# The order of state scans, head values and ScalarE activations in the mLSTM stretch, and early evictions into eight F buffers in all norms

## The chip, the core and the metric

One core of a Trainium2 chip runs the whole program. The metric is the device time in microseconds of one execution. The engines are TensorE (PE: matmul; PEld: its weight loads), VectorE (DVE), ScalarE (ACT), GpSimd (POOL) and SyncE (SP, which here only issues DMAs). Each engine runs its own instruction list in order, and they meet through semaphores. Matmuls write PSUM, of which this kernel uses eight banks of 128 x 512 f32.

## The reference

Two transformer blocks over 512 tokens of width 1024, in float32. The first one (sparse attention, retention, a squared-ReLU feed-forward) is touched by the change only in its two RMS norms. The second one is:

```
h   = standardize(x) * (1 + sc1) + sh1
xm, om, ip, fp, us, ga, gb = split(h @ w_in + b_in)
xc  = silu(causal_conv4(xm));  q, k = xc @ wq, xc @ wk;  v = xm        # 4 heads, 128 / 128 / 256
hm  = standardize(mlstm(q, k, v, ip, fp))                              # per head
y_a = (hm * gain * sigmoid(om)) @ w_down
ys  = gelu(s5_ssm(us));  val, gate = split(ys @ w_glu);  y_b = val * sigmoid(gate)
x   = layer_norm(alpha * x + (1 + g1) * ((sigmoid(ga) * y_a + sigmoid(gb) * y_b) @ w_mix_out))
h   = standardize(x) * (1 + sc2) + sh2
x   = layer_norm(alpha * x + (1 + g2) * conv_glu_ffn(h))
```

In the mLSTM, with m the running maximum of the gates, s = (q k^T) * exp(D - m) over past tokens, the head's value is (s v) / max(|sum of s|, exp(-m)). The S5 part is a linear state recurrence with 64 complex states for each of 32 groups.

## The kernel before, in words

**Weights.** All weight matrices are cut into 113 tiles of 128 x 2048 (1 MB), in the order of `CHUNKS` (L71). SP loads them into two `raw` slots (`tiles`, L2316; a load waits for the split of the tile two before). ACT rounds a tile to `whi` (`hi_upto`, L889: it waits for the load and for the last product of the tile two before; `take`, L901, splits up to one tile ahead of the product it then evicts). POOL subtracts, `wlo = raw - whi`, in four quarters (L1402). A product of 128 x 512 is then three matmuls for each 128 rows, with the activations split in the same way (`Ahi`/`Alo`, `Bhi`/`Blo`): `gemm` (L428) and `token_gemm` (L459).

**PSUM.** Three pools of banks go round: G (2, for `gemm`), T (4) and O (2). TensorE waits in `bank` (L415) until the user before has freed the bank (`taken`), and consumers wait for `full`.

**The norms.** There are four, s = 0 to 3. Per tile i of 128 tokens: statistics on DVE, square root on ACT (`root`, L907), the scale on DVE (`row_scale`, L1435), the scaled row `N` on ACT (`normed_row`, L913). TensorE turns the row into two banks (`normed_tile`, L453). ACT evicts each bank in four pieces with gain and bias into one of two F buffers (`scaled`, L923), and DVE splits the buffer into `Ahi` and `Alo` (`parts`, L1446). With two buffers an eviction waits for the `parts` of two evictions before (L930). In `normed_out` (L941) all four rows come first, then all evictions; norm 3 has its own loop (L1366 to L1375). In norms 1 and 2 (`rows_of`, L1718) and in norm 3 the rows end in the second half of a `token_gemm`, which sends tile 0's turns before its last piece (L510).

**The S5 part.** Projections `us0` to `us3` go through HBM into runs (`UG`); `run_inputs` (L736) feeds the scans on DVE (`run_states`, L2045, two halves); `run_outputs` (L751, two halves) adds 32 products with `TOEG` and 64 with the scanned states `xs`; `runs_out` (L1178) stores them as `y_runs`, `y_back` loads them as `YC`, `gelus` and DVE's `ys_part` make `YShi`/`YSlo`.

**The spilled projections.** 32 projections `xm`, `om`, `ga`, `gb` (k = 0 to 31) are computed, evicted (L1288), and stored to HBM (`spill`). The other work of the stretch hangs on their number k, in one list for TensorE (L831 to L857) and one for ACT (L1282 to L1343). TensorE: k = 2 `run_inputs`, k = 6 the `aec` transposes of the gate rows, k = 8 and 9 `run_outputs`. DVE's list is written out: `gate_rows` 1, 2, 3 (cumulative sums and maxima of the gates, L2015, with activations of ACT at k = 1, 2, 3 between them), then the two scans, then the heads (L2183 to L2203).

**A head** h starts at b = `HEAD_AT[h]`. On TensorE: k = b `mlstm_front` (the product `nb` and the turns of `XM` to `V`), b+1 `mlstm_qk`, b+2 `mlstm_scores`, b+3 `mlstm_values` (ten products of 256 columns into two O banks, and ten of one column, the denominator, into a T bank), b+5 `mlstm_back` (turns of `H`). On ACT: b+1 `head_in`, `head_qk`, `head_decay`; b+2 `load_so`; b+4 the `silus` of the next head's conv and then `head_rows` (the root and four scaled rows `H`); b+6 `head_high` (`Bhi`). On DVE: `weighted`, `head_low` of the head before, `conv` of the next, `values_out` (statistics and denominators), `conv_out` (`XCh`/`XCl`), `diagonal`, `head_out`.

**After them** come eight steps of `gv`, `gg`, `md` products; the first `md` waits for all of `Bhi`/`Blo`. ACT takes `gv` after DVE's `g8_free`. SP waits for all spills and `heads_done`, loads the gains of the norm, and then for each step two 256 KB gate tiles and one weight tile (L2398 to L2411).

Of the kernel before, what the change touches and what calls it, by code (L numbers as in the profile page):

```python
# [55 lines left out]
HEAD_AT = [13, 17, 22, 26]  # L56
# [105 lines left out]
def build(nc, d, out):  # L162
    ctx = ExitStack()
    with ctx:
# [184 lines left out]
        G2b = at("G2b", [P, D], offY)  # L349

# [61 lines left out]
        def _(pe):  # L412
# [46 lines left out]
            def token_gemm(name, hi, lo, kn, ready, turns=False, s=None):  # L459
# [323 lines left out]
            def mlstm_values(h):  # L783
# [3 lines left out]
                for p in range(2):  # L787
                    ps, where = bank("O")
                    for i in range(2 * p, 2 * p + 2):
                        for j in range(i + 1):  # L790
                            at_ = [0, 512, 896, 1152][j] + (i - j) * P
                            ins = pe.matmul(ps[:, i % 2 * ML_DV:(i % 2 + 1) * ML_DV], W[:, at_:at_ + P],  # L792
                                            V[:, j, 0:ML_DV], start=(j == 0), stop=(j == i))
                    done(ins, f"mn{h}.{p}", where)
                ps, where = bank("T")
                for i in range(NT):
                    for j in range(i + 1):
                        at_ = [0, 512, 896, 1152][j] + (i - j) * P
                        ins = pe.matmul(ps[:, i:i + 1], W[:, at_:at_ + P], V[:, j, ML_DV:ML_DV + 1],
                                        start=(j == 0), stop=(j == i))  # L800
                done(ins, f"den{h}", where)

            def mlstm_back(h):
                for p in range(2):
                    pe.wait_ge(*taken(f"mn{h}.{p}"))
# [25 lines left out]
            for k, name in enumerate(SPILLED):  # L831
# [5 lines left out]
                if k == 6:  # L837

                    pe.wait_ge(sem("ifr_ready"), T.due("ifr_ready"))
                    ps, where = bank("T")  # L840
# [44 lines left out]
        def _(act):  # L885
# [37 lines left out]
            def scaled(i, s):  # L923

                for x in range(2):
# [15 lines left out]
            def normed_out(s, more=None):  # L941

                for i in range(NT):
                    root(i, s)
                    normed_row(i, s)
                    if i == 1 and s:
                        hi_upto(more)
                if s == 0:
                    hi_upto(more)
                    act.wait_ge(sem("par_in"), A.due("par_in", 16))  # L950
                elif s == 2:
                    act.wait_ge(sem("mod_ready"), A.due("mod_ready"))
                for i in range(NT):
                    scaled(i, s)
# [257 lines left out]
            def head_in(h):  # L1212

                for c in range(2):
                    act.wait_ge(*full(f"v{h}.{c}"))
                    ps = bank_of(f"v{h}.{c}")
                    if h and c == 0:
                        act.wait_ge(*full(f"den{h - 1}"))
# [22 lines left out]
            def head_rows(h):  # L1241
# [7 lines left out]
                for i in range(NT):  # L1249
                    ps = bank_of(f"mn{h}.{i // 2}")  # L1250
                    ins = act.activation(H[:, i, :], ps[:, i % 2 * ML_DV:(i % 2 + 1) * ML_DV], ACT.Identity,
                                         scale=sd[:, i:i + 1], bias=nmr[:, i:i + 1])
                    if i % 2:
                        ins.then_inc(taken(f"mn{h}.{i // 2}")[0], 1)
# [27 lines left out]
            for k, name in enumerate(SPILLED + [""]):  # L1282
# [20 lines left out]
                if k == 2:  # L1303
# [3 lines left out]
                if k == 3:  # L1307
# [5 lines left out]
                if k == 8:  # L1313
# [11 lines left out]
                if k in (16, 18):  # L1325
                    gelus(k - 16)
                    gelus(k - 15)
# [1236 lines left out]
```

## Time and profile before

| | |
|---|---|
| median of 3 runs | 1675.78 us (1673.12 to 1678.27) |
| the profiled execution | 1674.36 us, its span 1672.4 us |
| mean granted TensorE clock | 0.945 |
| busy: PE, DVE, POOL, ACT | 91%, 53%, 38%, 35% |
| from 820 to 1140 us (S5 and mLSTM) | PE 289.6 of 320 us, clock 0.91 |

### The profile page before, as it was taken

The page shows a single profiled execution, that of the slowest core. Times are in us where ns is not written, and L with a number is a line of the kernel's source. Part 1 is how long each engine was busy: PE and PEld are TensorE (multiplying, and loading weights), DVE is VectorE, ACT ScalarE, POOL GpSimd, SP SyncE. Part 2 cuts the span into 40 slices and gives each one's busy share as a digit, 9 for nine tenths or more (in the row PEclk, how much of TensorE's full clock was granted, in tenths as well). Part 3 has the DMA queues.
Part 4 walks back from the last instruction along what each step waited for, and adds up shares of the span by engine and source line. Part 5 has one row for each costly group of instructions (what it writes and reads, how often), then busy time and mean ns, then how long its engine had stood idle before and what let it go on. Part 6 is the DMA issues. An engine that isn't in the chain of part 4 may idle for free. (4 is left out here: it accounts for less than half of the span.)

```text
span 1672.4 us, 19643 instructions
## 1 busy us (share of the span) xinstructions
PE 1525.9 (91%) x7216; PEld 1226.2 (73%) x7216; DVE 879.7 (53%) x1484; ACT 582.6 (35%) x856; POOL 643.0 (38%) x456
## 2 busy tenths in 40 slices
PE   4999989787999999997998999988994999999996
PEld 3776855676888788875877777777883888888885
DVE  4672378625858777397462255424548332333337
ACT  4332377115222121215341463444426332232231
POOL 2432200032655545562542224224551434544442
PEclk9999989898999999997997998998996999999998
DMA  7222000042655545222452633224421222223221
GB/s 273 88 92 78 26 26 2 1 164 97 212 189 198 205 151 189 101 76 82 113 149 78 173 103 131 89 87 171 138 76 76 76 101 101 84 93 105 97 101 51
DMA packets 48182, 185.72 MB, mean 111 GB/s; under 512 B 12960, under 2 KB 14112, under 8 KB 33248
## 3 DMA queue, kind: packets, MB, share of 16 engines
q1 hardware_dynamic: 30240, 165.53, 28.1%
q10 hardware_dynamic: 17856, 19.01, 4.1%
q8 instruction: 58, 0.95, 0.2%
q14 instruction: 28, 0.23, 0.0%
HBM read 169.71 MB, written 12.58 MB: 109 GB/s over the span
## 5 line engine op out<-in xcount | busy, mean ns | idle before, releaser
L1402 POOL TENSOR_TENSOR wlo<-raw,whi 128x512 fp32r<-128x512 f32 x448 | 637.3, 1453 | 997.0 <-ACT whi L898 997.0
L441 PE MATMUL bank<-Ahi,whi 128*128 128x512 f32 x1088 | 440.9, 405 | 22.0 <-issue 8.5
L442 PE MATMUL bank<-Alo,whi 128*128 128x512 f32 x1088 | 431.4, 397 | 0.0
L443 PE MATMUL bank<-Ahi,wlo 128*128 128x512 f32 x1088 | 431.2, 396 | 0.0
L898 ACT ACTIVATE whi<-raw 128x2048 fp32r<-128x2048 f32 x113 | 216.4, 1915 | 279.2 <-PE bank L471 216.9
L441 PEld LDWEIGHTS bank<-Ahi,whi 128*128 128x128 f32 x1088 | 210.1, 193 | 71.6 <-issue 17.4
L442 PEld LDWEIGHTS bank<-Alo,whi 128*128 128x128 f32 x1088 | 210.0, 193 | 45.1 <-issue 2.4
L443 PEld LDWEIGHTS bank<-Ahi,wlo 128*128 128x128 f32 x1088 | 208.9, 192 | 44.9
L469 PE MATMUL bank<-whi,Bhi 128*128 128x512 f32 x496 | 195.3, 394 | 5.6 <-POOL wlo L1402 5.6
L471 PE MATMUL bank<-whi,Blo 128*128 128x512 f32 x496 | 194.3, 392 | 0.0
L470 PE MATMUL bank<-wlo,Bhi 128*128 128x512 f32 x496 | 194.2, 392 | 0.0
L469 PEld LDWEIGHTS bank<-whi,Bhi 128*128 128x128 f32 x496 | 94.1, 190 | 27.0 <-POOL wlo L1402 7.4
L471 PEld LDWEIGHTS bank<-whi,Blo 128*128 128x128 f32 x496 | 93.8, 189 | 19.7
L470 PEld LDWEIGHTS bank<-wlo,Bhi 128*128 128x128 f32 x496 | 94.1, 190 | 19.2
L1742 DVE CUSTOM_DVE_ANT_0 junk<-adaw,cB 128x1024 f32<-128x1024 f32 x48 | 79.2, 1650 | 21.6 <-DMA adaw<-in_ada 16.6
L2283 DVE TENSOR_SCALAR FG<-GP,par 128x512 f32<-128x512 f32 x22 | 12.0, 546 | 147.8 <-ACT GP L1383 147.8
L450 PE MATMUL bank<-con,N 128*128 128x128 f32 x128 | 28.4, 381 | 49.9 <-ACT F L938 19.3
L1951 DVE TENSOR_TENSOR G<-G 128x512 f32<-128x512 f32 x32 | 33.4, 1044 | 62.3 <-ACT G L1114 62.3
L1288 ACT ACTIVATE stage<-bank,par 128x512 f32<-128x512 f32 x32 | 21.9, 684 | 125.7 <-PE bank L443 99.2
L1114 ACT ACTIVATE G<-bank 128x512 f32<-128x512 f32 x32 | 19.1, 598 | 130.4 <-PE bank L443 130.4
L450 PEld LDWEIGHTS bank<-con,N 128*128 128x128 f32 x128 | 20.7, 194 | 56.9 <-issue 43.9
L1466 DVE TENSOR_TENSOR X<-X,bank 128x512 f32<-128x512 f32 x40 | 27.5, 688 | 45.0 <-PE bank L471 43.9
(379 smaller groups left out, 1928.3 us busy)
## 6 DMA issues: line engine op xcount, KB each, us to landing
raw<-in_ws SPq DMA_DIRECT2D x113, 1024.0 KB, 5.0
adaw<-in_ada SPq DMA_DIRECT2D x48, 512.0 KB, 4.8
spill<-stage ACTq DMA_DIRECT2D x32, 256.0 KB, 2.0
X<-in_x SPq DMA_DIRECT2D x8, 512.0 KB, 6.2
gates<-spill SPq DMA_DIRECT2D x16, 256.0 KB, 2.9
w1k<-in_w1k SPq DMA_DIRECT2D x1, 2048.0 KB, 16.0
w1v<-in_w1v SPq DMA_DIRECT2D x1, 2048.0 KB, 20.2
XM<-spill ACTq DMA_DIRECT2D x8, 256.0 KB, 4.5
```

The source lines that it names most:

```text
L441: pe.matmul(ps[:], wh, hi[:, k], start=(k == 0), stop=False)
L442: pe.matmul(ps[:], wh, lo[:, k], start=False, stop=False)
L443: ins = pe.matmul(ps[:], wl, hi[:, k], start=False, stop=(k == kn - 1))
L450: ins = pe.transpose(ps[0:cols, i * width:i * width + rows], s, ident[0:rows, 0:rows])
L469: pe.matmul(ps[:], h, wh, start=(k == 0), stop=False)
L470: pe.matmul(ps[:], h, wl, start=False, stop=False)
L471: return pe.matmul(ps[:], l, wh, start=False, stop=stop)
L898: act.activation(whi[n % 2][:], raw[n % RAW][:], ACT.Copy).then_inc(sem("hi_split"), 1)
L1402: pool.tensor_tensor(wlo[slot][:, part], raw[slot][:, part], rd(whi[slot][:, part]), ALU.subtract).then_inc(sem("lo_split"), 1)
L1466: tt(x, x, ps[:], ALU.add).then_inc(taken(n)[0], 1)
L1742: dve.tensor_tensor_reduce(junk[:], adaw[t % 3][:], cB[:], 1.0, 0.0, ALU.mult, ALU.add, mod[:, t:t + 1]).then_inc(sem("ada_used"), 1)
L1951: tt(r[:], r[:], r[:], ALU.mult).then_inc(sem("dve_step"), 1)
```

## The change

Norms: eight buffers `FN` instead of two, at addresses free at that time. `scaled(i - 1)` follows `normed_row(i)` on ACT, the weight split comes after row 0 (norms 1, 2) or row 3 (norm 0), tile 0's turns are issued one piece earlier, DVE's `row_scale` of norm 0 follows the next tile's statistics, and norm 3 evicts three banks and splits tile 0 before its last row. mLSTM stretch: heads at 12, 17, 22, 27; scans before `gate_rows` 2 and 3, with ACT's part of them at k = 4 and 8 and `aec` at k = 9 (a bank of O) and 10; the wait for `xs_ready` behind the `TOEG` products; values and denominator in one product of 257 columns into a bank for each tile; `gelus` at 15 and 20, `head_rows` before `silus`, `ys_part` 2 and 3 after head 1's values; head 3's turn behind `gg0`, and one more weight tile loaded ahead of the spill wait.

```diff
-HEAD_AT = [13, 17, 22, 26]
+HEAD_AT = [12, 17, 22, 27]
...
+        firsts = {0: [offU + 2048 * q for q in range(8)], 1: [offX8 + 4096 + 2048 * q for q in range(8)]}
+        firsts[2] = firsts[1]
+        firsts[3] = [offU, offU + 2048] + [offU + 6144 + 2048 * q for q in range(6)]
+        FN = [[at(f"FN{n}_{q}", [P, S], firsts[n][q]) for q in range(8)] for n in range(4)]
...
             def token_gemm(name, hi, lo, kn, ready, turns=False, s=None):
...
-                    if turns and (q, i) == (1, 2):
+                    if turns and (q, i) == (1, 1):
                         normed_tile(s, 0)
...
             def run_outputs(half):
...
-                    pe.wait_ge(sem("xs_ready"), T.due("xs_ready"))
...
+                if half == 0:
+                    pe.wait_ge(sem("xs_ready"), T.due("xs_ready"))
                 for k in ks:
...
             def mlstm_values(h):
...
-                for p in range(2):
-                    ps, where = bank("O")
...
                 for i in range(NT):
+                    ps, where = bank("O" if i < 2 else "T")
                     for j in range(i + 1):
                         at_ = [0, 512, 896, 1152][j] + (i - j) * P
-                        ins = pe.matmul(ps[:, i:i + 1], W[:, at_:at_ + P], V[:, j, ML_DV:ML_DV + 1],
+                        ins = pe.matmul(ps[:, 0:ML_DV + 1], W[:, at_:at_ + P], V[:, j, :],
                                         start=(j == 0), stop=(j == i))
-                done(ins, f"den{h}", where)
+                    done(ins, f"mn{h}.{i}", where)
...
             for k, name in enumerate(SPILLED):
...
-                if k == 6:
+                if k == 9:
                     pe.wait_ge(sem("ifr_ready"), T.due("ifr_ready"))
-                    ps, where = bank("T")
+                    ps, where = bank("O")
...
                 gemm(f"gg{n}", YShi, YSlo)
                 if n == 0:
+                    mlstm_back(ML_H - 1)
                     pe.wait_ge(sem("B_ready"), T.due("B_ready", 8))
...
-            def scaled(i, s):
+            def scaled(i, s, halves=(0, 1)):
...
-                    if i:
-                        act.wait_ge(sem("A_ready"), 8 * s + 2 * (i - 1) + x + 1)
-                        f, p4 = Fb[x][:, c * P:(c + 1) * P], ps[:, c * P:(c + 1) * P]
+                        f, p4 = FN[s][2 * i + x][:, c * P:(c + 1) * P], ps[:, c * P:(c + 1) * P]
...
             def normed_out(s, more=None):
...
-                    if i == 1 and s:
+                    if i == 0 and s:
                         hi_upto(more)
...
+                    if i == NT - 1 and s == 0:
+                        hi_upto(more)
+                    if i:
+                        scaled(i - 1, s)
+                scaled(NT - 1, s)
...
             for k, name in enumerate(SPILLED + [""]):
...
-                if k == 2:
+                if k == 4:
                     act.wait_ge(sem("if_d"), A.due("if_d"))
                     act.activation(gr[0][0:4], IF[32:36], ACT.Copy).then_inc(sem("if_a"), 1)
-                if k == 3:
+                if k == 8:
                     act.wait_ge(sem("if_d"), A.due("if_d"))
                     act.activation(gr[0][0:4], gr[0][0:4], ACT.Exp).then_inc(sem("ifr_ready"), 1)
-                if k == 8:
+                if k == 10:
                     act.wait_ge(*full("aec"))
...
-                if k in (16, 18):
-                    gelus(k - 16)
-                    gelus(k - 15)
+                if k in (15, 20):
+                    gelus(0 if k == 15 else 2)
+                    gelus(1 if k == 15 else 3)
...
-                    if k == b + 6 or (k == len(SPILLED) and b + 6 >= k):
+                    if k == b + 6:
                         head_high(h)
...
                     if k == b + 4:
+                        head_rows(h)
                         if h < ML_H - 1:
                             silus(h + 1)
-                        head_rows(h)
+            hi_upto(last_tile(INDEX["gv0"]) + 1)
+            head_high(ML_H - 1)
...
                 normed_row(i, 3)
...
-            for i in range(NT):
-                scaled(i, 3)
+                if i == 1:
+                    scaled(0, 3)
+                if i == 2:
+                    scaled(1, 3, (0,))
+            scaled(1, 3, (1,))
+            scaled(2, 3)
+            scaled(3, 3)
...
                 row_stats(i, True)
-                row_scale(i, True)
+                if i:
+                    row_scale(i - 1, True)
+            row_scale(NT - 1, True)
...
-            for part in (1, 2, 3):
-                gate_rows(part)
+            gate_rows(1)
...
             run_states(0)
+            gate_rows(2)
             run_states(1)
             dve.sem_inc(sem("xs_ready"), 1)
+            gate_rows(3)
...
             def values_out(h):
...
+                    dve.wait_ge(*full(f"mn{h}.{i}"))
+                    ps = bank_of(f"mn{h}.{i}")
+                    den_ = ps[:, ML_DV:ML_DV + 1]
+                    ts(dd[:, i:i + 1], den_, -1.0, AEC[:, 1, i, h:h + 1], ALU.mult, ALU.max).then_inc(sem("dve_step"), 1)
+                    dve.bn_stats(st4[:, i, 0, :], ps[:, 0:ML_DV])
+                    dve.wait_ge(sem("dve_step"), v.did("dve_step"))
+                    ins = tt(dd[:, 4 + i:5 + i], dd[:, i:i + 1], den_, ALU.max)
...
                 values_out(h)
-                if h == 0:
-                    ys_part(0)
-                    ys_part(1)
+                if h < 2:
+                    ys_part(2 * h)
+                    ys_part(2 * h + 1)
...
-                if h == 0:
-                    ys_part(2)
-                    ys_part(3)
...
             dve.sem_inc(sem("gb_used"), 1)
+            parts(3, 0)
             again_scale(NT - 1)
-            for i in range(NT):
+            for i in range(1, NT):
                 parts(3, i)
...
-            n_heads = n_s5
+            n_heads = n_s5 + 1
+            tiles(n_s5, n_heads)
             whole_spill()
```

## Rows read from the trace of the kernel before

**Rows 1.** Stretches: length, busy time of PE, PEld, DVE, ACT, POOL, granted clock, DMA
```profile
883.09:888.62 5.53, 0.00 (x0) 0.03 (x1) 5.30 (x5) 0.77 (x2) 3.51 (x3) 0.68 0.29 76
...
888.62:902.64 14.02, 14.02 (x97) 13.78 (x97) 0.00 (x0) 0.00 (x0) 0.00 (x0) 0.50 0.16 65
...
902.64:909.54 6.90, 6.90 (x26) 5.60 (x25) 0.00 (x0) 0.00 (x0) 0.00 (x0) 0.79 0.00 0
...
916.87:933.49 16.62, 16.61 (x74) 13.44 (x72) 0.09 (x3) 2.64 (x5) 0.37 (x1) 1.00 0.61 139
...
909.54:916.87 7.33, 7.33 (x97) 7.19 (x95) 0.00 (x0) 2.48 (x2) 4.57 (x4) 1.00 0.09 36
...
935.72:943.07 7.35, 7.35 (x25) 5.63 (x25) 4.84 (x4) 3.60 (x3) 5.53 (x4) 0.77 0.53 167
...
962.05:1118.11 156.06, 147.52 (x663) 119.01 (x662) 70.96 (x142) 76.69 (x107) 49.51 (x36) 0.93 0.28 95
...
1124.50:1134.55 10.05, 0.00 (x0) 0.03 (x1) 0.00 (x0) 2.47 (x3) 0.50 (x1) 0.64 0.99 373
```

**Rows 2.** Timeline of DVE: start, length, the first instruction of the scans
```profile
857.85 0.69 DVE L2053 TENSOR_TENSOR zz<-bank,ctab 128x512 f32<-128x512 f32 x1
```

**Rows 3.** Who TensorE waited for, 820 to 1140 us
```profile
PE bank L450 <- ACT H L1251: 6.2, 3, 2.2
...
PE bank L441 <- DVE XCl L2107: 1.6, 1, 1.6
...
PE bank L441 <- ACT QK L1239: 0.8, 1, 0.8
```

**Rows 4.** Timeline and one source line: tile 69, and the `Blo` of the heads
```profile
1120.59 1.42 DVE L2180 TENSOR_TENSOR Blo<-F,Bhi 128x512 fp32r<-128x512 f32 x2 [0.24 <-DVE F L2171]
...
L2180 DVE TENSOR_TENSOR Blo<-F,Bhi x8: 693/1476/1666, 1006.8 to 1121.3; 128x512 fp32r<-128x512 f32 x8
...
1132.06 1.91 ACT L898 ACTIVATE whi<-raw 128x2048 fp32r<-128x2048 f32 x1 [10.92 <-DMA raw<-in_ws]
```

**Rows 5.** Timeline: projection 10's eviction, the first conv, head 0's last `XCl`
```profile
922.64 0.69 ACT L1288 ACTIVATE stage<-bank,par 128x512 f32<-128x512 f32 x1 [10.41 <-PE bank L443]
...
938.16 0.94 DVE L2003 TENSOR_SCALAR CA<-XM,par 128x512 f32<-128x512 f32 x1 [21.02 <-DMA XM<-spill]
...
949.05 0.69 DVE L2107 TENSOR_TENSOR XCl<-CA,XCh 128x512 fp32r<-128x512 f32 x1
```

**Rows 6.** Source line L1207, the `silus`: duration min/median/max in ns
```profile
L1207 ACT ACTIVATE CA<-CA x8: 632/633/635, 946.4 to 1077.2; 128x512 f32<-128x512 f32 x8
...
L1207 ACT ACT_TABLE_LOAD  x4: 1283/1283/1283, 938.1 to 1075.3; - x4
```

**Rows 7.** Chain of waits: head 3's value products and one-column products
```profile
1100.65 4.32 PE bank L792 x20
...
1104.97 2.12 PE bank L799 x20
```

**Rows 8.** Norms: `parts` by source line, evictions, each norm's first projection
```profile
L1456 DVE TENSOR_TENSOR Alo<-F,Ahi x32: 692/693/1639, 20.8 to 1294.4; 128x512 fp32r<-128x512 f32 x32
...
16.21 1.15 ACT L917 ACTIVATE N<-X,sd 128x1024 f32<-128x1024 f32 x1 [0.30 <-DVE sd L1438]
...
402.72 0.77 PE L441 MATMUL bank<-Ahi,whi 128*128 128x512 f32 x1 [3.98 <-issue]
...
759.32 1.09 PE L450 MATMUL bank<-con,N 128*128 128x128 f32 x8
...
780.13 0.77 PE L441 MATMUL bank<-Ahi,whi 128*128 128x512 f32 x1 [4.66 <-DVE Alo L1456]
...
1282.43 11.44 ACT L938 ACTIVATE F<-bank,mod 128x128 f32<-128x128 f32 x32
...
1293.83 0.77 PE bank L441
```

**Rows 9.** DMA issues: the gate loads, and their median time to landing
```profile
gates<-spill SPq DMA_DIRECT2D x16, 256.0 KB, 2.9
```

More of the change, by code:

```diff
@@ L786, in mlstm_values @@
                 pe.wait_ge(sem("mw_ready"), T.due("mw_ready", NT))
-                for p in range(2):
-                    ps, where = bank("O")
[L789 to L794, printed above, removed]
-                ps, where = bank("T")
                 for i in range(NT):
+                    ps, where = bank("O" if i < 2 else "T")
                     for j in range(i + 1):
                         at_ = [0, 512, 896, 1152][j] + (i - j) * P
-                        ins = pe.matmul(ps[:, i:i + 1], W[:, at_:at_ + P], V[:, j, ML_DV:ML_DV + 1],
+                        ins = pe.matmul(ps[:, 0:ML_DV + 1], W[:, at_:at_ + P], V[:, j, :],
                                         start=(j == 0), stop=(j == i))
-                done(ins, f"den{h}", where)
+                    done(ins, f"mn{h}.{i}", where)
             def mlstm_back(h):
-                for p in range(2):
-                    pe.wait_ge(*taken(f"mn{h}.{p}"))
+                for i in range(NT):
+                    pe.wait_ge(*taken(f"mn{h}.{i}"))
                 for c in range(2):
@@ L836, in _ @@
                     run_outputs(k - 8)
-                if k == 6:
+                if k == 9:
                     pe.wait_ge(sem("ifr_ready"), T.due("ifr_ready"))
-                    ps, where = bank("T")
+                    ps, where = bank("O")
                     for x in range(2):
@@ L921, in normed_row @@
                 ins.then_inc(sem("norm_rows"), 1)
-            def scaled(i, s):
-                for x in range(2):
+            def scaled(i, s, halves=(0, 1)):
+                for x in halves:
                     n = f"xT{s}.{i}.{x}"
@@ L945, in normed_out @@
                     normed_row(i, s)
-                    if i == 1 and s:
+                    if i == 0 and s:
                         hi_upto(more)
[L948 to L952, printed above, removed]
-                for i in range(NT):
-                    scaled(i, s)
+                    if i == 0 and s == 0:
+                        act.wait_ge(sem("par_in"), A.due("par_in", 16))
+                    if i == 0 and s == 2:
+                        act.wait_ge(sem("mod_ready"), A.due("mod_ready"))
+                    if i == NT - 1 and s == 0:
[3 more added lines that the diff above has]
+                scaled(NT - 1, s)
             def through(name):
@@ L1217, in head_in @@
                     if h and c == 0:
-                        act.wait_ge(*full(f"den{h - 1}"))
+                        act.wait_ge(*full(f"mn{h - 1}.{NT - 1}"))
                     act.activation(V[:, :, c * P:(c + 1) * P], ps[:].rearrange("p (i c) -> p i c", i=NT),
@@ L1249, in head_rows @@
                 for i in range(NT):
[L1250 to L1254, printed above, removed]
+                    n = f"mn{h}.{i}"
+                    act.activation(H[:, i, :], bank_of(n)[:, 0:ML_DV], ACT.Identity, scale=sd[:, i:i + 1],
+                                   bias=nmr[:, i:i + 1]).then_inc(taken(n)[0], 1)
             def head_high(h):
@@ L2132, in values_out @@
                 for i in range(NT):
[L2133 to L2139 removed]
+                    dve.wait_ge(*full(f"mn{h}.{i}"))
[5 more added lines that the diff above has]
+                    ins = tt(dd[:, 4 + i:5 + i], dd[:, i:i + 1], den_, ALU.max)
+                ins.then_inc(sem("dve_step"), 1)
                 dve.wait_ge(sem("dve_step"), v.did("dve_step"))
[L2141 to L2142 removed]
                 dve.reciprocal(dd[:, 4:8], dd[:, 4:8]).then_inc(sem("dve_step"), 1)
@@ L2272, in _ @@
             dve.sem_inc(sem("gb_used"), 1)
+            parts(3, 0)
             again_scale(NT - 1)
-            for i in range(NT):
+            for i in range(1, NT):
                 parts(3, i)
```

11 lines of the change are left out of this document (1 added, 10 removed).

## The prediction

> **What bounds the kernel now.** The page first: TensorE is busy 91% of the span, every other engine at most 53%. So time can only come from three places: where TensorE waits, where it runs at its lower clock, and work of its own that is removed. The table of stretches gives all three for the region the change touches. The chain of waits says who ended each wait, and the timeline says what stood in that engine's queue.
>
> The dearest place is the state scan. After the first `om` projection TensorE waits 5.53 us for `xs_ready`. Then the 96 small products of `run_outputs(0)` take 14.02 us at a granted clock of 0.50, where the same work in `run_outputs(1)` takes 7.33 us at 1.00. The projection after them needs 6.90 us instead of 5.54 (16.62 us for three at full clock) [rows 1]. Behind it: DVE starts the scans at 857.85 though the products that feed the first scan end at about 847, because all three `gate_rows` parts stand in front of them [rows 2].
>
> From head 0's values to the last spilled projection, 156.06 us hold 147.52 us of work [rows 1]: 8.5 us are waits. Most end on `H` (6.2 us, three heads), two short ones on `XCl` and `QK` [rows 3]. After them TensorE repeats instructions at half rate (the clock of the stretch is 0.93). I count about 8.6 us of that: 29 wide matmuls at 0.43 instead of 0.23 us, and some 3 us on turns and products. Before the first `md` product it waits 10.05 us for a G bank [rows 1]: ACT takes `gv0` only after splitting tile 69, whose load SP issues after `heads_done` [rows 4].
>
> **The sum, part by part**, against the profiled execution of 1674.4 us (median of the runs: 1675.8, so 1.4 us above it).
>
> 1. *Scans before gate rows 2 and 3, the skip products ahead of the `xs_ready` wait.* The scan of a half costs at most 17 us (871.8 to 888.5, half of it beside POOL) and gate rows 2 at most 4. From 847 this gives `xs_ready` at 876 to 885. TensorE asks for it at 882.4 + 3.5 = 886 (the end of projection 8 less the 0.66 of the `aec` transposes, which move behind it, and half of `run_outputs`). ACT's new wait at projection 4 for the cumulative sum ends near 864, before projection 5 is complete (865.9). Its wait at projection 8 for gate rows 3 ends by 890, while TensorE is in `run_outputs(0)`; the transposes that need it come at about 903. So the wait goes, and the clock stays up: 5.53 + (14.02 - 7.33) + (6.90 - 5.54) = **-13.6**.
> 2. *Head 0 one projection earlier (13 to 12).* This adds a wait. ACT issues the loads of `XM` behind eight `y_runs` stores; they land 15.5 us after projection 10 ended (922.6 to 938.16) [rows 5], and nothing of this moves. TensorE now wants `XM` 11.9 us after it: two projections of 5.5, one product of 0.9. It waits 3.9 us. Then it has one projection before it needs `XCl`, 27 us after projection 10 (949.7) [rows 5]: 3.2 us more. Each wait is followed by a stretch at the low clock, 1.5 to 1.8 us lost (today, after a wait of 2.23, the projection from 935.72 took 7.35 instead of 5.54 [rows 1]). Lost 10.2, against 4.4 that this stretch loses now: **+5.8**. Ends: 0 and +12 (both waits twice as long).
> 3. *`silus` behind `head_rows`, heads 5 projections apart.* `H` comes 2.6 us earlier (a table load of 1.28 and two activations of 0.63 [rows 6]), and ACT needs 4.9 us from the full projection to `H` (eviction 0.7, table load 1.28, root 0.2, DVE's scale and mean 0.8, four rows 1.9) where TensorE computes 5.5. The scaled `CA` comes later, but `mlstm_qk` is now a projection further off. New: `head_high` stands in front of `V` and `QK` at three hand-overs, some 1.0 us each like today's 0.8 [rows 3]. Head 3's hand-over and head 2's rows have a weight split (1.9) in front too, 1.9 and 1.2. With 1 to 2 us of low clock, 7 of the 17 us stay: **-10**. Ends: 0 and -17.
> 4. *The 257th column in the value products.* The ten one-column products cost 2.12 us a head on the chain, ten of 256 columns 4.32 [rows 7]; one column more is 0.4% of that. 4 x 2.1 = **-8.4**. `values_out` gets about 0.9 us longer on DVE; it has 17 us between the scores and the root and needs 11 to 16 for weights, `head_low` and conv, 4 for itself. It hides, just. No row has 257 columns: if the form needed a second pass, 4 x 4.3 = +17, the other end.
> 5. *Tile 69 before the spill wait, head 3 turned back behind `gg0`.* The load and split are now done early. What is late next is `B_ready`: from the turn of head 3 at 1118.0 it takes 4 us (to 1122.0), up to 5.5 now, because POOL splits tile 69 meanwhile and the two `Blo` subtractions cost 1.6 each instead of 0.7 [rows 4]. Then `g8_free` releases `gv0`. `md0` starts 5.5 + 1.0 (the turn) + 4.5 + 0.7 (`gv0`) = 11.7 us after `gb7` instead of 16.4: **-4.7**. Ends: -1 and -7.
> 6. *The norms.* Eight buffers take away the ping-pong of ACT and DVE over two. In norm 3, 12 of 32 evictions move ahead of the last row; 20 of 0.36 us are left after it, but `parts(3, 0)` pushes that row back 0.8: start 1290.3 instead of 1293.83 [rows 8], **-3.6**. In norm 1 the last row comes at 392.3 and DVE has seven halves of 1.17 us to split: 400.5 instead of 402.72, **-2.2**. In norm 2 ACT serves 32 evictions of 0.36 us in any order, and TensorE reaches the early `normed_tile` before its row exists: it idles from 756.4 to 759.3 and loses clock: 780.5 instead of 780.13 [rows 8], **+0.4**. In norm 0 `row_scale(0)` waits for the second tile's statistics, row 3 comes at 19.6 instead of 16.2, and the splits of tiles 0 and 1 fall into the time of `parts`. Beside a POOL subtraction DVE's 0.69 us takes 1.64 [rows 8], and a cast and subtraction together 3.0 instead of 1.17. I take three halves at 3 us: 34.8 instead of 31.75, **+3**, ends -1.5 and +4. Together **-2.4**.
>
> The row shows that DVE and POOL stretch each other. The Trainium skill (SBUF - State Buffer, Who interferes with whom) says why: a VectorE instruction with two SBUF inputs and a GpSimd one that reads SBUF exclude each other for the whole instruction, first come, first served. By that rule, with the longer POOL instruction first each time, norm 0 would cost the +4 end; with DVE first, little.
>
> Sum: -13.6 + 5.8 - 10 - 8.4 - 4.7 - 2.4 = -33.3, so **1641 us**.
>
> **The rivals.**
> A: *the forecast*, 1641, chance 0.62.
> B: *the head stretch stays chained.* ACT and DVE pass `XM`, `CA`, `V`, `QK`, `H` in an order just as tight as before, and every wait over 2 us costs low clock after it. Steps 2, 3 and 5 then give +12, 0 and -1: -13.6 + 12 + 0 - 8.4 - 1 - 2.4 = -13, 1661; half of that way is 1651. For it: the conv of head 1 took 10 us beside POOL, and DVE has under 1 us to spare there. Against: most waits had `silus` or a load in front of them. Chance 0.16.
> C: *the `XM` wait does not come, and the hand-overs clear.* Step 2 gives 0, step 3 -17: 1628. For it: today's stretch there loses 4.4 us for a similar cause. Against: the loads' place in ACT's queue is not changed. Chance 0.15.
> D: *257 columns double the value products*: 1641 + 17 = 1658. The present products already read `V` with rows of 257 elements at full rate. Chance 0.04.
> E: *slower.* SP's loop now issues `tiles(n_heads + n)` one tile further, so the pair of gate loads for step n + 1 stands behind a wait for the split of tile 68 + n. If that split came after the gates are needed, each of the 8 gated steps would pay a landing of 2.9 us [rows 9], a sigmoid of 1.05 and 1.8 of low clock: 8 x 5.8 = +46, 1687. It decides once the split of tile 68 + n ends later than `g8_free` of the step before. The split is asked for with `gv` of step n - 1, about when `g8_free` of n - 2 comes, and the windows from 1160 to 1240 have TensorE busy throughout. Chance 0.03.
>
> The range is 1628 to 1656: it takes in C and half of B, and leaves out its far end, D and E. A measurement of this kernel can tell about 0.3%, 5 us, from no change. A, C and D are faster by more; of B's 0.16 I give 0.02 to no change and 0.01 to slower, should its waits be worse than drawn. With E: faster 0.94, same 0.02, slower 0.04.
>
> **What would show it.** Step 1: no wait at the skip products and `run_outputs(0)` at clock 1.00 in about 7.4 us. Step 2: a wait of about 4 us ended by the `XM` load, and one of 3 us by `XCl`. Step 3: no wait on `H`, short ones on `QK`. Step 4: 80 product records of 257 columns (0.38 us each), no one-column ones. Step 5: no wait on tile 69, about 5 us before `md0`. Step 6: first projections at about 35 us in norm 0, 2 us earlier after norm 1, 3.6 after norm 3, unchanged after norm 2. The forecast is wrong if TensorE still waits over 2 us at each hand-over, or if the `XM` wait is missing.

## The result, and the profile after

The changed kernel takes 1645.08 us (median of four runs, 1643.17 to 1652.11), the kernel before 1677.03 beside it. The ratio is 0.9819, 95% interval 0.9801 to 0.9838: 30.4 us faster (27.2 to 33.4), where 33.3 was the sum. The profiled execution took 1643.61 us, its span is 1641.7, against 1674.36 and 1672.4.

The stretches of the changed kernel that answer to [rows 1]: length, busy time of PE, PEld, DVE, ACT, POOL, granted clock, DMA.
```profile
886.06:893.46 7.40, 7.40 (x98) 7.26 (x96) 6.64 (x4) 2.60 (x3) 6.54 (x4) 1.00 0.56 177
893.46:898.96 5.50, 5.50 (x24) 4.54 (x25) 0.00 (x0) 0.00 (x0) 0.00 (x0) 1.00 0.57 194
898.96:906.36 7.40, 7.40 (x98) 7.26 (x97) 0.00 (x0) 3.77 (x3) 3.31 (x3) 1.00 0.09 35
...
930.03:936.79 6.76, 6.76 (x24) 5.11 (x23) 6.44 (x7) 0.38 (x1) 3.38 (x3) 0.80 0.31 101
...
951.94:1100.85 148.91, 142.29 (x628) 113.72 (x627) 71.46 (x166) 78.59 (x109) 47.90 (x36) 0.99 0.33 114
1101.88:1106.79 4.91, 0.00 (x1) 0.03 (x1) 4.25 (x5) 2.28 (x5) 4.49 (x3) 1.00 0.00 0
```
The 96 products of `run_outputs(0)` now take 7.40 us at full clock with no wait ahead of them (14.02 at 0.50 before), the projection behind them 5.50 (6.90). The fifth row runs from head 0's scores to head 3's turn, with one projection more than the long row of [rows 1] and the two products of `gv0` and `gg0`: it lies at clock 0.99 instead of 0.93. The last row is the wait before the first `md` product, 4.91 instead of 10.05.

Who TensorE waited for, 820 to 1140 us (us in total, times, longest), against [rows 3]:
```profile
PE bank L445 <- DVE Blo L2185: 4.9, 1, 4.9
PE bank L750 <- DMA UG<-u_runs: 3.9, 1, 3.9
PE bank L454 <- DMA XM<-spill: 3.5, 1, 3.5
PE bank L445 <- DVE XCl L2113: 3.1, 1, 3.1
PE bank L454 <- ACT H L1249: 2.7, 1, 2.7
PE bank L445 <- ACT QK L1237: 2.7, 3, 1.1
PE bank L445 <- ACT stage L1284: 1.2, 1, 1.2
```
The waits on `XM` and `XCl` that step 2 priced are there, and of the three on `H` one is left. The products of one head's values (each product with 257 columns leaves two records, so ten of them are x20), and from the timeline the first projection behind each norm and the one new wait, in norm 2:
```profile
L796 PE MATMUL bank<-V,W x20: 377/380/383, 1085.5 to 1089.6; 128*128 128x257 f32 x20
```
```profile
35.10 0.80 PE L445 MATMUL bank<-Ahi,whi 128*128 128x512 f32 x1 [12.70 <-DVE Alo L1459]
...
407.32 0.76 PE L445 MATMUL bank<-Ahi,whi 128*128 128x512 f32 x1 [5.25 <-issue]
...
761.66 1.66 PE L454 MATMUL bank<-con,N 128*128 128x128 f32 x8 [2.29 <-ACT N L917]
...
782.97 0.76 PE L445 MATMUL bank<-Ahi,whi 128*128 128x512 f32 x1 [5.27 <-DVE Alo L1459]
...
1263.08 0.76 PE L445 MATMUL bank<-Ahi,whi 128*128 128x512 f32 x1 [4.39 <-issue]
```

### The profile page after: what moved, and what is told of

Its sections match the earlier page's. It is cut to its first block and busy times, and to the rows that moved or that the text cites. A ratio compares the mean times of both kernels' runs of the same rounds, so it can differ in the third digit from the quotient of the medians.

```text
span 1641.7 us, 19484 instructions
## 1 busy us (share of the span) xinstructions
PE 1502.7 (92%) x7136; PEld 1208.2 (74%) x7136; DVE 890.2 (54%) x1508; ACT 582.4 (35%) x857; POOL 645.4 (39%) x456
## 5 line engine op out<-in xcount | busy, mean ns | idle before, releaser
L454 PE MATMUL bank<-con,N 128*128 128x128 f32 x128 | 24.8, 356 | 40.2 <-ACT N L917 20.6
L1284 ACT ACTIVATE stage<-bank,par 128x512 f32<-128x512 f32 x32 | 21.9, 684 | 86.8 <-PE bank L447 63.6
```

The source lines that it names most:

```text
L454: ins = pe.transpose(ps[0:cols, i * width:i * width + rows], s, ident[0:rows, 0:rows])
```

## The experiments

Each kernel was timed in five rounds beside the kernel before on the same chip, and chips differ between groups. So ratios are compared, and differences in us are ratios times 1677 us.

**The four parts, each alone on the kernel before.**

`norms_only` is the hunks of the norms. 

> The kernel before with the norms' part of the change alone (FN buffers, evictions behind each row, early turns, late row_scale of norm 0). My sum: -2.4 us against before (norm 0 +3, norm 1 -2.2, norm 2 +0.4, norm 3 -3.6), so 1673 to 1674 us. The two traces so far show something that the sum has no term for: from the first projection (31.75 before, 35.10 after) to wout the changed kernel loses 2.9 us more in code that nothing touches. If that belongs to the late start of norm 0 (the clock falls at other places), it shows here too: the stretch from the first projection to wout takes 309.1 us instead of 306.2, and the whole is +0.5 rather than -2.4. If it comes with the mLSTM part (which is later in time, so it could only be chance), this stretch takes 306.2 as before.

Measured: 0.9979 (0.9964 to 0.9994), -3.5 us. Norm 0 starts the first projection at 35.69 (+3.9), norm 1 gives 1.7, norm 2 costs 0.35, norm 3 gives 3.5 (all from the start of the work that leads to the norm, against the same distance before), together -0.9. From the first projection to `wout` it takes 307.2 us: neither the 309.1 of the one theory nor the 306.2 of the other. What ten profiles say of this stretch stands further down.

`scans_only`:
```diff
-            for part in (1, 2, 3):
-                gate_rows(part)
+            gate_rows(1)
...
             run_states(0)
+            gate_rows(2)
             run_states(1)
             dve.sem_inc(sem("xs_ready"), 1)
+            gate_rows(3)
```
with ACT's steps at k = 4 and 8, `aec` behind projection 9, and the `xs_ready` wait behind the `TOEG` products. 

> The kernel before with the scans ahead of gate rows 2 and 3, ACT's gate steps at k = 4 and 8, aec behind projection 9, and the xs_ready wait behind the TOEG products; nothing else. Parts add up: -13.6 us, 1662 us; no wait before the scanned-state products, run_outputs(0) at clock 1.00. Rival (the time is given back later, since the heads and y_runs then come at the same distance behind DVE's shorter slack): -8 us or less, with longer waits on XM, XCl and H than the kernel before has.

Measured: 0.9916 (0.9899 to 0.9933), -14.1 us; parts add up. `run_outputs(0)` of this kernel and the projection behind it, in the table of stretches:
```profile
887.04:894.44 7.40, 7.40 (x98) 7.26 (x96) 6.65 (x4) 2.60 (x3) 6.55 (x4) 1.00 0.56 178
894.44:899.94 5.50, 5.50 (x25) 4.54 (x25) 0.00 (x0) 0.00 (x0) 0.00 (x0) 1.00 0.56 194
```
The waits at the heads are as before (6.1 us on `H`): nothing is given back.

`values_only`:
```diff
-                            ins = pe.matmul(ps[:, i % 2 * ML_DV:(i % 2 + 1) * ML_DV], W[:, at_:at_ + P],
-                                            V[:, j, 0:ML_DV], start=(j == 0), stop=(j == i))
+                        ins = pe.matmul(ps[:, 0:ML_DV + 1], W[:, at_:at_ + P], V[:, j, :],
+                                        start=(j == 0), stop=(j == i))
```
with a bank for each of the four sums, two of O and two of T. 

> The kernel before with the 257-column value products alone (and what reads them: values_out, head_rows). Parts add up: 4 x 2.1 = -8.4 us, 1667 us. Rival (the hand-overs behind it are bound by DVE and ACT, not by TensorE): the four H waits grow by what TensorE saves, 2 us each, and the whole gains under 2 us.

Measured: 1.0024 (1.0009 to 1.0038), 4.0 us slower (1.5 to 6.4), worse than either theory. The products did become 2.1 us shorter for each head. Who TensorE waited for in this kernel, and from its timeline ACT's rows of head 0 and the turn of head 1's second bank of `V`:
```profile
PE bank L450 <- ACT H L1243: 17.1, 3, 7.4
```
```profile
987.68 1.93 ACT L1243 ACTIVATE H<-bank,nmr,sd 128x256 f32<-128x256 f32 x4 [0.77 <-DVE nmr L2150]
...
989.20 1.11 PE L450 MATMUL bank<-con,XM 128*128 128x128 f32 x4 [7.39 <-ACT H L1243]
```
Look at the tile: it is the turn of `XM` that waits, and what ends the wait is a row of `H` of the head before. Of the four T banks two now hold `mn0.2` and `mn0.3` until these rows are written; `nb1` and `v1.0` take the other two, and `v1.1` has none. It happens where heads are 4 projections apart: at head 1 and at head 3, 7.4 us each. The prediction priced the products and DVE's longer `values_out`, not the banks.

`heads_tail_only` is `HEAD_AT` 12, 17, 22, 27, `head_rows` before `silus`, `gelus`, `ys_part`, head 3's turn and tile 69. 

> The kernel before with HEAD_AT 12, 17, 22, 27, head_rows before silus, gelus at 15 and 20, ys_part 2 and 3 after head 1, head 3's turn behind gg0 and tile 69 ahead of the spill wait. My steps 2, 3 and 5: +5.8 - 10 - 4.7 = -8.9 us, 1667 us. Rival (the steps need the scans' and the values' part to work, because the one-column products and the late y_runs give DVE and ACT time): the sum of the four parts run singly is then less than the -30.7 us of the whole change by over 5 us.

Measured: 0.9991 (0.998 to 1.0002), -1.5 us. Apart from the 5.5 us for `xs_ready`, the waits are nearly those of the changed kernel (2.6 on `H`, 2.4 on `XM`, 4.2 on `XCl`, 4.9 on `Blo`), so steps 2 and 5 are at work, and still almost nothing is won. The four parts singly give -3.5 - 14.1 + 4.0 - 1.5 = -15.1, half of the -30.4 of the whole. So it came as the rival has it.

**Heads, tail and values together.** `heads_values` has the last two, without norms and scans. 

> The kernel before with the heads', the tail's and the values' part, without the scans and the norms. Singly the heads' and tail's part brought -1.5 us and the values' part +4. The trace of the values' part alone shows why it lost: mn2 and mn3 now sit in two of the four T banks until the rows of H are written, and with heads 4 projections apart the second turn of V (head 1 and head 3) waits for such a bank, 7.4 us each. It also shows TensorE at full clock after the products (two projections in 11.28 us instead of 12.77). Theory of the bank: with heads 5 apart both waits go, and each head gives 2.1 + 1.5 us: -1.5 - 4 x 3.6 = -16 us, about 1661 us, no gap at a turn of V. Rival (parts add): +2.5 us, 1679 us.

Measured: 0.9914 (0.9898 to 0.993), -14.4 us, where the two singly sum to +2.5. No turn of `V` waits. Norms, scans and this: -3.5 - 14.1 - 14.4 = -32.0, the whole within its interval. So the missing half lay between these two parts. The stretch from head 0's first scores to the wait before the first `md` product, in the kernel before, `values_only`, `heads_tail_only`, `heads_values` and the changed kernel:
```profile
959.97:1124.49 164.52, 155.98 (x699) 125.32 (x697) 75.45 (x149) 80.43 (x110) 49.51 (x36) 0.94 0.29 100
```
```profile
962.56:1127.90 165.34, 145.15 (x619) 115.25 (x617) 75.79 (x173) 80.54 (x110) 48.52 (x36) 0.93 0.28 98
```
```profile
964.02:1131.26 167.24, 160.77 (x723) 129.65 (x721) 70.02 (x144) 81.44 (x110) 47.76 (x36) 0.95 0.30 106
```
```profile
961.37:1116.41 155.04, 148.39 (x643) 117.71 (x641) 72.74 (x168) 81.54 (x110) 47.84 (x36) 0.97 0.32 114
```
```profile
949.63:1101.88 152.25, 145.63 (x643) 116.03 (x641) 72.75 (x168) 81.56 (x110) 47.90 (x36) 0.99 0.33 116
```
The last three hold one projection (5.5 us) more. Length less PE's busy time gives the waits; the granted clock while PE is busy gives what its lower level costs (1 less the clock, times the time); the products are 8.4 us shorter in three of the five.

| us | length, without the extra projection | waits | lost at the lower clock | products |
|---|---|---|---|---|
| before | 164.5 | 8.5 | 9.6 | |
| `values_only` | 165.3 | 20.2 | 7.2 | -8.4 |
| `heads_tail_only` | 161.7 | 6.5 | 8.5 | |
| `heads_values` | 149.5 | 6.7 | 4.8 | -8.4 |
| changed | 146.7 | 6.6 | 1.7 | -8.4 |

Singly the two parts change the length by +0.8 and -2.8, together by -15.0, which is 13 us more than their sum. Of these 13 the waits are 11.5: the two turns of `V` that wait for a bank in `values_only` are not there when the heads are 5 apart. The clock is the other 1.3, and of it one profile each is weak evidence, as the next rows show. First `heads_tail_only`, whose first row is the end of head 0's products with the ten of one column, then `heads_values`:
```profile
975.50:978.20 2.70, 2.70 (x24) 2.62 (x24) 0.77 (x2) 2.38 (x3) 2.70 (x3) 1.00 0.00 0
978.20:981.00 2.80, 2.80 (x9) 2.25 (x9) 1.38 (x10) 0.00 (x0) 0.65 (x1) 0.59 0.29 82
981.00:984.00 3.00, 3.00 (x12) 2.40 (x12) 0.00 (x0) 0.00 (x0) 0.00 (x0) 0.81 0.65 273
```
```profile
973.50:976.00 2.50, 2.50 (x13) 2.02 (x12) 2.32 (x10) 1.82 (x2) 2.50 (x3) 1.00 0.00 0
```
Behind the one-column products the granted clock falls to 0.59, with no wait near it, and nine matmuls stand in 2.8 us where the other kernel has 13 in 2.5; behind the 257-column products it stays at 1.00. Two projections take 12.75 us there and 11.28 here. In the profile of `heads_tail_only` this happens behind all four heads, in those of the kernel before and of `scans_only` behind head 1 alone, in that of `norms_only`, whose heads are those of the kernel before, behind heads 0 and 1: eight of sixteen heads. Behind the 257-column products of ten kernels, forty heads, it never happens. So the one-column form is what the eight have in common, but that the spacing of the heads brings it out is not shown, since the number differs without a change of spacing too, and what decides it stays open. From the start of the values to the turn of `H` head 0 is 3.8 us shorter (19.06 against 15.28), not 2.1.

The Trainium skill (TensorE: Matmul & The Clock Gate, Part 1) says that a monitor sets TensorE's clock by how busy the engine has been. By the records it was busy for all of the 2.70 us ahead of the fall; that the clock can fall behind a busy time of tiny products is what these rows add.

**Where head 0 starts.** On the changed kernel:
```diff
-HEAD_AT = [12, 17, 22, 27]
+HEAD_AT = [13, 17, 22, 27]
```

> The changed kernel with HEAD_AT 13, 17, 22, 27 instead of 12, 17, 22, 27. My step 2 (the early head 0 costs 5.8 us through the waits for XM and XCl): these two waits shrink to the 2.2 and 0.9 us of before, -5 us against the changed kernel. Theory of the bank: heads 0 and 1 are then 4 apart, so the second turn of V of head 1 waits 3 to 5 us for a T bank, and what is won at XM is given back: -1 to +2 us against the changed kernel (0.981 to 0.983 of before).

Measured: 0.9828 (0.9812 to 0.9844) against 0.9819, +1.5 us: no gain. Its waits, 900 to 1145 us:
```profile
PE bank L454 <- ACT H L1249: 8.5, 2, 5.8
PE bank L445 <- DVE Blo L2185: 4.9, 1, 4.9
PE bank L445 <- ACT stage L1284: 4.3, 3, 2.4
```
The waits on `XM` and `XCl` are gone, as step 2 has it; 5.8 us at head 1's second turn take their place, the bank again. So the theory of the bank (-1 to +2) held and step 2's -5 did not. With the last head at 27, whose rows of `H` follow the last projection, heads 5 apart begin at 12: the 5 us of step 2 are the price of the spacing.

**Loading `XM` ahead of the `y_runs` stores.**
```diff
                 for q in range(4):
                     act.wait_ge(*taken(f"yrun{q}"))
+                load_xm(0)
                 for j in range(STEPS):
                     act.dma_start(y_of_step[j], YG[S5_C * j:S5_C * j + S5_C, :, :]).then_inc(sem("y_out"), 16)
...
                 if k == 10:
                     runs_out()
-                    load_xm(0)
                     load_xm(1)
```

> The changed kernel with the loads of head 0's XM issued behind the YG activations and ahead of the eight y_runs stores. ACT's queue shows the stores issued from 915.5 to 922.3 and the XM loads at 922.4; they would be issued at 915.5 and land about 7 us earlier, before TensorE wants them at 924.5. Both waits (3.5 for XM, 3.1 for XCl) go with the low clock behind them: -7 to -10 us against the changed kernel (about 0.977 of before). Rival: the stores then land later and the y_back loads or the gelus push DVE and ACT, so that the wait moves to H or QK of head 0 or 1: under -3 us.

Measured: 0.9776 (0.9762 to 0.9791), -7.2 us against the changed kernel. The first conv starts at 918.41 instead of 928.11, with projection 10 at the same place within 1 us:
```profile
914.80 1.00 ACTq L1268 DMA_DIRECT2D XM<-spill  x2
...
918.41 0.55 DVE L2008 TENSOR_SCALAR CA<-XM,par 128x512 f32<-128x512 f32 x1 [12.52 <-DMA XM<-spill]
```
TensorE no longer waits for `XM`; for `XCl` it still does (2.85 us, where the expectation had none). So the place of the loads in ACT's queue was the cause of the wait on `XM` that step 2 foresaw. From projection 10 to head 0's first scores the traces give 37.9 instead of 42.8 us, -4.8; the rest of the -7.2 is within what the two intervals leave open.

**Norm 0 in another order.**
```diff
-                    if i == 0 and s == 0:
-                        act.wait_ge(sem("par_in"), A.due("par_in", 16))
...
-                    if i == NT - 1 and s == 0:
-                        hi_upto(more)
-                    if i:
+                    if i and s:
                         scaled(i - 1, s)
+                if s == 0:
+                    act.wait_ge(sem("par_in"), A.due("par_in", 16))
+                    for i in range(NT - 1):
+                        scaled(i, s)
+                    hi_upto(more)
                 scaled(NT - 1, s)
```
and DVE's `row_scale(i)` behind its own tile's statistics again, on top of `xm_first`. 

> xm_first, and norm 0 in another order: DVE's row_scale right behind each tile's statistics as before the change, ACT writes all four rows first, then evicts tiles 0 to 2, splits the weight, and evicts tile 3. Row 3 comes at about 16.2 again and POOL's subtraction starts only when most of DVE's splits are done, so the first projection starts at 28 to 31 us instead of 35.1: -4 to -7 us against xm_first (0.973 to 0.975 of before). Rival (what delays norm 0 is the evictions and splits themselves, one behind the other, not the order): 33 us or later, -2 us or less.

Measured: 0.9726 (0.9712 to 0.9741), -8.4 us against `xm_first`. The timeline of the changed kernel, then of this one: one of DVE's splits, POOL's first subtraction, another split, and here the first projection.
```profile
22.06 0.69 DVE L1459 TENSOR_TENSOR Alo<-FN,Ahi 128x512 fp32r<-128x512 f32 x1
...
22.26 3.02 POOL L1405 TENSOR_TENSOR wlo<-raw,whi 128x512 fp32r<-128x512 f32 x2 [21.81 <-ACT whi L896]
...
24.20 1.63 DVE L1459 TENSOR_TENSOR Alo<-FN,Ahi 128x512 fp32r<-128x512 f32 x1
```
```profile
24.67 0.69 DVE L1460 TENSOR_TENSOR Alo<-FN,Ahi 128x512 fp32r<-128x512 f32 x1
...
25.18 4.42 POOL L1406 TENSOR_TENSOR wlo<-raw,whi 128x512 fp32r<-128x512 f32 x3 [24.73 <-ACT whi L896]
...
26.81 1.64 DVE L1460 TENSOR_TENSOR Alo<-FN,Ahi 128x512 fp32r<-128x512 f32 x1
...
28.50 0.79 PE L445 MATMUL bank<-Ahi,whi 128*128 128x512 f32 x1 [6.10 <-DVE Alo L1460]
```
In the changed kernel three banks are split before POOL's work stretches DVE's and four beside it, at 3.07 us each from 22.79; here six are split before and one beside it. The first projection starts at 28.50 instead of 35.10 (35.64 in `xm_first`). The edit changes two things at once: of the 6.6 us, 1.0 comes from the splits starting earlier (18.27 instead of 19.23, since the rows are no longer held back) and the rest from three fewer stretched ones. This fits the rule that the prediction took from the Trainium skill (SBUF - State Buffer, Who interferes with whom): each subtraction beside POOL takes 1.63 instead of 0.69, and the one at 22.06, which began before POOL's, keeps its 0.69. The cast, which has one SBUF input and of which that rule does not speak, is stretched too, from 0.43 to 1.37.

**Tile 69.** The changed kernel with the load and the split of tile 69 late again, head 3's turn still behind `gg0`:
```diff
-            hi_upto(last_tile(INDEX["gv0"]) + 1)
             head_high(ML_H - 1)
...
-            n_heads = n_s5 + 1
-            tiles(n_s5, n_heads)
+            n_heads = n_s5
```

> The changed kernel without the early load and split of tile 69 (SP loads it behind heads_done again, ACT splits it only with gv0); head 3's turn stays behind gg0. My step 5: the wait before the first md product grows from 4.9 to about 10 us, +4.7 us against the changed kernel (0.985 of before). Rival (the turn behind gg0 alone is what shortened the wait): under +1 us.

Measured: 0.9875 (0.9849 to 0.99), +9.4 us. The wait, and what it hangs on in the timeline:
```profile
PE bank L445 <- issue: 15.4, 1, 15.4
```
```profile
1105.66 0.53 SPq L2332 DMA_DIRECT2D raw<-in_ws  x1
...
1113.58 1.91 ACT L896 ACTIVATE whi<-raw 128x2048 fp32r<-128x2048 f32 x1 [10.75 <-DMA raw<-in_ws]
```
The wait is 5.3 us longer than before the change, not equal to it: `heads_done` comes behind head 3's turn, the turn has moved back by `gv0` and `gg0`, and the load of the tile waits for `heads_done`. The later turn without the early tile is a loss of about 5 us against the kernel before (21.9 us from `gb7` to `md0`, 16.4 before); only with the tile loaded early does it pay.

**ACT's order at head 0 and at the hand-overs.** `silu_early`, on `xm_first_norm0`:
```diff
-                if k == 12:
+                if k == 11:
                     silus(0)
```

> xm_first_norm0 with silus(0) on ACT behind projection 11's eviction instead of projection 12's, ahead of a weight split. In xm_first_norm0 the conv of head 0 ended at 916.6, but ACT reached the silu only at 919.9, and TensorE waited 2.9 us for XCl at 923.3. Theory: XCl is complete at about 922.5, the wait and the 1.5 us of low clock behind it go: -4 us against xm_first_norm0 (0.970). Rival (the split and POOL's subtraction come 2.6 us later and projection 12 or 13 waits for the weights): 0.

Measured: 0.9752 (0.9733 to 0.9771), +4.4 us against 0.9726, the intervals overlapping; in the profiles, from projection 10 to head 0's first scores, 38.7 against 37.8 us. So at best nothing: the wait on `XCl` went, and 0.53 and 0.86 on `stage` and 2.64 on `QK` came, which are waits for ACT as well.

`combined`:
```diff
-                    if k == b + 6:
-                        head_high(h)
                     if k == b + 1:
                         head_in(h)
                         head_qk(h)
+                        if h:
+                            head_high(h - 1)
...
                         head_rows(h)
+                        hi_upto(last_tile(INDEX[name]) + 1)
```
and the other edits that its expectation lists. 

> silu_early, and on ACT: head_high of the head before behind head_qk instead of ahead of it, the weight splits at k = 26 and 28 behind the rows of H and behind head_decay, the split of tile 69 behind head_high(3) (its load stays early), and norm 2's tile 0 turned behind piece (1, 2) again. Of the waits that remain in xm_first_norm0: QK 0.77, 0.77 and 1.13, H 2.71 (should fall to 0.8), stage 1.24, Blo 4.91 (should fall to about 3.9), and 1.5 to 2.5 us of low clock behind the wait on H; norm 2 0.5 us. Theory: each wait was set by what stands in front on ACT: -8 us against silu_early (0.965). Rival (DVE's side of the hand-over sets them, or a split comes too late for TensorE): -2 us or less.

Measured: 0.968 (0.9659 to 0.9702), -12.1 us against `silu_early`, which the expectation of -8 names, and -7.7 against `xm_first_norm0`. From the first scores to the first `md` product it is 149.9 us instead of 158.6, so -8.7 of it lies where the edits act. Its waits, 900 to 1145 us:
```profile
PE bank L445 <- issue: 4.7, 1, 4.7
PE bank L445 <- ACT QK L1244: 2.7, 1, 2.7
PE bank L445 <- POOL wlo L1417: 1.7, 1, 1.7
PE bank L445 <- ACT stage L1297: 1.5, 2, 0.9
PE bank L454 <- ACT H L1256: 0.3, 1, 0.3
```
The waits of heads 1 to 3 on `QK` and `H` are gone. In their place stands one on POOL at projection 29, whose weight split had been put too late; the one before the first `md` product hardly moved (4.66 for 4.91).

`combined_2` has `silus(0)` at 12 again and this split ahead of `head_decay(3)`. 

> combined with silus(0) behind projection 12 again, and the weight split of projection 28 between head_high(2) and head_decay(3) instead of behind head_decay(3). In combined POOL's first quarter of the tile came late by 1.74 us at projection 29 and the early silu left waits of 0.59, 0.87 and 2.66 in place of the one for XCl. Theory: the wlo wait goes without one on QK or W in its place, and the start of head 0 is 1 us better: -2 to -3.5 us against combined (0.966). Rival (the split in front of head_decay makes E late, so that W and the value products wait): 0 or slower.

Measured: 0.969 (0.9667 to 0.9713), the same as `combined`. The wait on POOL is gone and 0.8 us on `E` came, and head 0's start has three waits of 1.0, 1.4 and 1.5. Either kernel is 3.1 to 3.2% faster than the one before and 1.3 to 1.4% faster than the changed one.

## Why the prediction came out right, and where its steps did not

The forecast said 1641, the median is 1645.08, inside the range. The sum was 2.9 us too large against the times. The mechanisms of steps 1, 2 and 5 are those that the experiments show; steps 3 and 4 came out only as a pair, for reasons that the prediction did not have, and that the whole came so near is in part luck.

Step 1 held: -13.8 us in the trace (73.0 us from `run_inputs` to projection 10 before, 59.2 after) for -13.6, and -14.1 alone. `xs_ready` came 38.3 us after the start of `run_inputs`; my bounds, 876 to 885 in the time of the kernel before, are 32.1 to 41.1 us after it. TensorE asked for it 3.7 us later.

Step 2 held: waits of 3.5 and 3.1 us where I gave 3.9 and 3.2, +5.2 for +5.8. What it called the cost of an earlier head 0 is the cost of heads 5 apart, and the place of the `XM` loads is the cause of the first of its two waits.

Steps 3 and 4 held as a pair and failed singly. From the first scores to the first `md` product, the extra projection and step 5 set aside, the traces give about -18 (174.6 us before, 157.2 after) for -18.4. But in `heads_tail_only` step 3 alone brought 3 us there, not 10, and step 4 alone made `values_only` 4.0 us slower, not 8.4 faster. Two terms failed. Step 3 put the low clock of the stretch down to the waits ("With 1 to 2 us of low clock, 7 of the 17 us stay"). By the table the waits fell only from 8.5 to 6.5 us, and the loss at the lower clock from 9.6 to 8.5 with step 3 alone: in that profile the clock falls behind the one-column products of all four heads, some 1.5 us each, which only step 4 takes away. And step 4 counted instructions without asking how long the new sums hold their T banks (14.8 us of waits at two turns of `V`); the cover it named was DVE's alone.

That the pair met its sum within 0.4 us is luck. `heads_values` has the same heads and gives -15 in the same stretch. The difference is what follows one wait: the wait on `H` is 2.7 us in both, and in the ten microseconds behind it 1.7 us are lost at the lower clock in the changed kernel and 4.8 in `heads_values` (1.7 to 3.4 in six more kernels with this wait). Nor do the profiles of the three kernels with the heads as before agree on the stretch: 174.6, 172.6 (`norms_only`) and 171.3 us (`scans_only`).

Step 5: -4.95 us (16.44 to 11.5 from `gb7` to `md0`) for -4.7, by the chain I gave, `Blo` last. That the load "is now done early" carries all of it: without it the later turn turns the step into a loss.

Step 6: +3.35, -1.65, +0.5 and -3.1 us for +3, -2.2, +0.4 and -3.6, together -0.9 for -2.4 in the trace. One term was missing. From norm 1's first projection to the start of the last token product before norm 2, the nine profiles with the new norms take 308.4 to 309.7 us and the five with the old ones 310.8 to 311.7. That is 2.3 us less in the changed kernel, and it brings the norms to -3.2, beside the -3.5 (-1.0 to -6.0) of `norms_only`. Which edit of the norms brings it stays open.

The changed kernel also took 2.9 us more from the first projection to `wout`, where no edit is. In the five profiles with the old norms, whose code is the same up to there, this stretch takes 306.2 (the kernel before), 309.9, 307.9, 310.8 and 307.8 us; in the five with the norm 0 of the changed kernel 307.2, 309.1, 307.3, 304.9 and 307.3. So executions of equal code differ by over 4 us there, and the profile of before was the quickest of its five. The 2.9 us need no cause in the change.

Of the rivals, B and D did not come: the waits did not chain, and a product of 257 columns costs what one of 256 did (0.377 to 0.383 us a record; 0.377 to 0.379 before). B's premise, that every wait over 2 us costs low clock after it, does not hold either: in `scans_only` a wait of 2.2 us on `H` is followed by 10 us at 1.00. C was wrong on `XM`. E did not come: from the first `md` product to `mix` it is 86.45 us after and 86.33 before.

## What to carry to other kernels

Two edits that each look like a gain can be worth nothing or less alone and a lot together: ask of every edit how long it holds a buffer of a shared pool, and which other edit gives that time. When such a change is priced, run its parts singly and in pairs; here four parts gave half of the whole and one pair the rest. Before a step of the sum is called right to a tenth, look at the same stretch in a second profile: here it moved by 3 us without an edit. On an engine that issues its DMAs in its own order, put the load that the next stage waits for ahead of the stores that nobody waits for (4.8 us here by the traces, 7.2 by the times), and start a weight split beside which VectorE would be stretched only when VectorE is nearly done (6.6 us at the first projection, 1.0 of them by the earlier rows).

## What the runs showed of the hardware

Ten one-column products in 2.1 us, with PE busy throughout by the records, were followed by a granted clock of 0.59 and 0.81 in the next 6 us in `heads_tail_only`: 1.5 us lost, on top of the 2.1 they take. It happened behind 8 of 16 heads in four kernels, and behind none of 40 heads with products of 257 columns. A record of a 257-column product in f32 lasts 0.38 us, as one of 256 did, and the twenty of a head 4.51 us (4.49 with 256), with the clock at 1.00 behind them. What a wait costs in clock differs between profiles: behind a wait of 2.6 to 2.7 us on `H`, 1.7 to 4.8 us were lost within 10 us, and behind one of 2.2 us 0, 1.7 or 3.3 us. A stretch of 306 to 311 us of equal code differed by 4.6 us between five profiles, so a difference of 3 us between two profiles, in a stretch that holds no edit, is not a finding.
